# Seven block products instead of eight for nearly all hidden tiles of three FFNs, with the weight sums made by DMA in DRAM

## The reference, cut to what matters

```python
def swiglu_half(x, g, w_up, w_down):
    h = rmsnorm(x, g)
    gate, up = jnp.split(h @ w_up, 2, axis=-1)
    return x + 0.5 * ((jax.nn.silu(gate) * up) @ w_down)

for l in range(DEPTH):
    x = swiglu_half(x, p['ffn1_norm'][l], p['ffn1_w_up'][l], p['ffn1_w_down'][l])
    y, st = mixer(rmsnorm(x, p['mix_norm'][l]), l, lb_all[l], p, tuple(s[l] for s in states))
    x = x + y
    x = swiglu_half(x, p['ffn2_norm'][l], p['ffn2_w_up'][l], p['ffn2_w_down'][l])
```

## Time and profile before

| | |
|---|---|
| Time, median of 3 runs | 3029.66 us (3028.21 to 3030.39) |
| Profiled execution | 3033.17 us, span 3031.4 us |
| TensorE | 2964.1 us busy, 98%, 23664 matmuls |
| VectorE | 1602.5 us busy, 53% |
| ScalarE | 786.5 us busy, 26% |
| GpSimd | 1752.3 us busy, 58% |
| DMA | 271.22 MB, 89 GB/s |

### The profile page before, as it was taken

One profiled execution on the slowest core, in us unless ns is written; L12 is line 12 of the kernel. 1 busy time (PEld: TensorE's weight loads), 2 busy tenths in 40 slices (PEclk: granted clock), 3 DMA queues, 4 the chain that ended last, 5 costly groups with the idle time before them and its releaser, 6 DMA issues.

```text
span 3031.4 us, 65367 instructions
## 1 busy us (share of the span) xinstructions
PE 2964.1 (98%) x23664; PEld 2876.5 (95%) x23664; DVE 1602.5 (53%) x2155; ACT 786.5 (26%) x1296; POOL 1752.3 (58%) x1604
## 2 busy tenths in 40 slices
PE   7999999999999999999999999999999999999998
PEld 7999999989988999999999999999898889999998
DVE  7563665535323467364674736745353245673646
ACT  4221232031232324131241312321303323331212
POOL 5666575545543575656666665654545445766665
PEclk9999999999999999999999999999999999999999
DMA  3232232232221332222232221322312123322231
GB/s 135 79 111 87 70 127 77 67 106 68 82 70 60 106 118 100 88 86 101 74 105 84 90 98 65 125 71 66 114 63 86 63 75 112 108 89 101 80 108 68
DMA packets 115174, 271.22 MB, mean 89 GB/s; under 512 B 9240, under 2 KB 53152, under 8 KB 114720
## 3 DMA queue, kind: packets, MB, share of 16 engines
q1 hardware_dynamic: 65088, 231.76, 22.7%
q10 hardware_dynamic: 49888, 36.71, 4.0%
HBM read 249.92 MB, written 18.52 MB: 89 GB/s over the span
## 4 chain that ended last, share of the span: by engine, by line
PE 88%; DVE 6%; issue 2%; ACT 2%; POOL 1%; ACTq 0%; DMA 0%; PEld 0%; DVEq 0%; POOLq 0%
PE dense L536 64%; PE SA L584 8%; PE SB L584 6%; PE SA L712 1%; PE SA L797 1%; PE SA L698 1%; PE SA L641 1%; PE SA L781 1%; PE SB L793 1%; DVE tmp L1241 1%; DVE Hl L1246 1%; POOL Wl L484 0%; PE SA L683 0%; PE SA L784 0%; PE SA L630 0%
## 5 line engine op out<-in xcount | busy, mean ns | idle before, releaser
L482 POOL TENSOR_SCALAR Wh<-raw 128x512 fp32r<-128x512 f32 x740 | 542.5, 733 | 1037.2 <-PEq L541 935.5
L484 POOL TENSOR_TENSOR Wl<-raw,Wh 128x512 fp32r<-128x512 f32 x740 | 1021.2, 1380 | 61.7
L536 PE MATMUL dense<-Hh,Wh 128*128 128x272 f32 x3104 | 663.0, 295 | 23.6 <-DVE Hl L1232 10.1
L536 PE MATMUL dense<-Hh,Wl 128*128 128x272 f32 x3104 | 648.4, 291 | 0.0
L536 PE MATMUL dense<-Hl,Wh 128*128 128x272 f32 x3104 | 647.9, 290 | 0.0
L536 PEld LDWEIGHTS dense<-Hh,Wh 128*128 128x128 f32 x3104 | 493.7, 191 | 34.8 <-issue 17.6
L536 PEld LDWEIGHTS dense<-Hl,Wh 128*128 128x128 f32 x3104 | 494.9, 191 | 0.0
L536 PEld LDWEIGHTS dense<-Hh,Wl 128*128 128x128 f32 x3104 | 492.9, 192 | 0.0
L536 PE MATMUL dense<-Ah,Wh 128*128 128x272 f32 x1408 | 290.9, 288 | 4.7 <-DVE Al L1333 4.7
L536 PE MATMUL dense<-Ah,Wl 128*128 128x272 f32 x1408 | 289.5, 288 | 0.0
L536 PE MATMUL dense<-Al,Wh 128*128 128x272 f32 x1408 | 289.2, 287 | 0.0
(11 more groups left out here) (423 smaller groups left out, 5246.9 us busy)
## 6 DMA issues: line engine op xcount, KB each, us to landing
raw<-wst SPq DMA_DIRECT2D x336, 512.0 KB, 3.3
pair<-wst SPq DMA_DIRECT2D x80, 512.0 KB, 4.0
raw<-wst SPq DMA_DIRECT2D x32, 384.0 KB, 2.9
x_keep<-X ACTq DMA_DIRECT2D x2, 2176.0 KB, 8.3
X<-x_keep ACTq DMA_DIRECT2D x16, 272.0 KB, 3.1
sst<-st_h ACTq DMA_DIRECT2D x8, 512.0 KB, 4.5
s_h<-sst ACTq DMA_DIRECT2D x8, 512.0 KB, 3.4
sst<-st_c ACTq DMA_DIRECT2D x8, 512.0 KB, 4.0
```

Source lines behind the costliest of these rows:

```text
L482: pool.tensor_scalar(Wh[:, j, cs], raw[:, j, cs], 1.0, 0.0, ALU.mult, ALU.add).then_inc(glink, 1)
L484: pool.tensor_tensor(Wl[:, j, cs], raw[:, j, cs], f32(Wh[:, j, cs]), ALU.subtract).then_inc(glink, 1)
L536: mm = pe.matmul(dps[slot][:, a, 0:HALF], w[:, ring, w0:w0 + 128], x[:, k, a * HALF:(a + 1) * HALF], start=(k == 0 and n == 0), stop=(k == ...
```

## The change

FFN 0 stays as it was, but for signs: the sums of activations and weights are taken with other signs, and the combination adds or subtracts accordingly. In FFNs 1, 2 and 3 all 20 hidden tiles after the first two are computed with seven products, back to back in groups of 6, 8 and 6 between the tiles of w_down.

For these FFNs VectorE makes no weight sums. Three of the four sums (called W1, W2, W3 here, for S1, S2, S3) are made in a DRAM tensor `w_sums` by DMA transfers that GpSimd issues: per chunk of 6 or 8 hidden tiles three copies and three adding transfers, for FFN 1 during FFN 0, for FFN 2 during the mixer of layer 0, for FFN 3 during that of layer 1. They run on two counters, and GpSimd waits for the last transfer of a counter before it issues the next on it. The sum of all four blocks (S4) is made by GpSimd in SBUF from A12 and S2. SyncE loads A11, A12, S1 and S2 (two transfers of 512 KB) when the five rests of VectorE of the last pair are made, and S3 and A22 (two of 256 KB) when the two rests of GpSimd are. VectorE makes five rests per pair, GpSimd two and the sum. The rounding and the rests of the next pair are put between the steps that combine this pair's products (`products`). The first pair of FFNs 1 and 3 is prepared during the tiles of w_out, that of FFN 2 at the end of FFN 1. The loop over the layers is written out, in Python, on all engines.

The core of the diff (of functions with two versions, the order is SyncE, GpSimd, TensorE, ScalarE, VectorE):

```diff
-FAST = FF_TILES // 2 - 1
+HALF_FAST, FAST = FF_TILES // 2 - 1, FF_TILES - 2
+EXTRA = 2 * (FAST - HALF_FAST)
 FFN_TILES = FFN_PIECES - 2 * FAST
+FFN1_T0 = (-EXTRA, 0)
 UP_AT = (2, 18, 34)
-DOWN_AT = (10, 26, 40)
-FAST_AT = (-1, 3, 7)
+HALF_AT = (-1, 3, 7)
+DOWN_AT = ((4, 12, 20), (10, 26, 40))
+FAST_AT = (0, FF_BLOCK - 2, 2 * FF_BLOCK - 2, FAST)
...
+            def load_seven(f, i):
+
+                if i in FAST_AT:
+                    chunk = 3 * (f - 1) + FAST_AT.index(i) + 1
+                    sp.wait_ge(sum_s, 16 * SUM_S * chunk)
+                    sp.sem_inc(pair_began, 1)
+                    sp.wait_ge(sum_r, 16 * SUM_R * chunk)
+                    sp.sem_inc(pair_began, 1)
+                at, n = gate_piece(f, i), (f - 1) * FAST + i
+                sp.wait_ge(q_lo, ONE + LOW0[f] + i * DVE_LO)
+                sp.sem_inc(pair_began, 1)
+                if n:
+                    sp.wait_ge(sum_four, n)
+                    sp.sem_inc(pair_began, 1)
+                sp.dma_start(pair[:, 0:4:3, :], wst[at, :, :].rearrange("p (a c) -> p a c", a=2)).then_inc(first_in, 16)
+                sp.dma_start(pair[:, S2:S1 + 1, :], w_sums[0:2, n, :, :].rearrange("s p c -> p s c")).then_inc(
+                    first_in, 16)
+                sp.wait_ge(q_lo_pool, ONE + POOL0[f] + i * POOL_LO)
+                sp.dma_start(wsum[:, 0, :], w_sums[2, n, :, :]).then_inc(second_in, 16)
+                sp.dma_start(wsum[:, 2, :], wst[at + 1, :, 512:1024]).then_inc(second_in, 16)
...
+            def ffn(f, p0, d0):
+                for t in range(4):
+                    load(p0 + t, d0 + t, t % 2)
+                load_seven(f, 1)
+                for b, nf in enumerate((FF_BLOCK, FF_BLOCK, FF_LAST)):
+                    for m in range(KT):
+                        if m == 2:
+                            for i in range(FAST_AT[b] + 2, min(FAST_AT[b + 1] + 2, FAST)):
+                                load_seven(f, i)
+                            if b == 2 and f == 1:
+                                load_seven(f + 1, 0)
+                        load(p0 + DOWN_AT[0][b] + m, d0 + 24 * b + 2 * nf + m, m % 2, nf * P)
...
+                    if p == MIX_PIECES - 4:
+                        sp.wait_ge(mix_clear, L + 1)
+                        sp.sem_inc(pair_began, 1)
+                        load_seven(2 * L + 1, 0)
...
+            def sums(f, c):
+
+                i0, i1 = FAST_AT[c // SUM_OPS], FAST_AT[c // SUM_OPS + 1]
+                at, n0, n1 = gate_piece(f, i0), (f - 1) * FAST + i0, (f - 1) * FAST + i1
+                blocks = wst[at:at + 2 * (i1 - i0), :, :].rearrange("(n u) p (h c) -> u h p n c", u=2, h=2)
+                G_a, U_a, U_b = blocks[0, 0], blocks[1, 0], blocks[1, 1]
+                W2, W1, W3 = (w_sums[s, n0:n1, :, :].rearrange("n p c -> p n c") for s in range(3))
+                F2, F1 = (flat(w_sums[s, n0:n1, :, :]) for s in range(2))
+                op = c % SUM_OPS
+                if op in (3, 5):
+                    if sent["r"]:
+                        pool.wait_ge(sum_r, 16 * sent["r"])
+                        pool.sem_inc(sum_began, 1)
+                    if op == 3:
+                        pool.dma_start(W3, G_a).then_inc(sum_r, 16)
+                    else:
+                        pool.dma_start(W3, U_a, accum_op=ALU.add).then_inc(sum_r, 16)
+                    sent["r"] += 1
+                    return
+                if sent["s"]:
+                    pool.wait_ge(sum_s, 16 * sent["s"])
+                    pool.sem_inc(sum_began, 1)
+                if op == 0:
+                    pool.dma_start(W1, U_a).then_inc(sum_s, 16)
+                elif op == 1:
+                    pool.dma_start(W1, U_b, accum_op=ALU.add).then_inc(sum_s, 16)
+                elif op == 2:
+                    pool.dma_start(F2, F1).then_inc(sum_s, 16)
+                else:
+                    pool.dma_start(W2, G_a, accum_op=ALU.add).then_inc(sum_s, 16)
+                sent["s"] += 1
...
+            def lows(f, i):
+
+                n = PAIR0[f] + i - HALF_FAST
+                pool.wait_ge(first_in, n * 32 + 32)
+                pool.sem_inc(sum_began, 1)
+                pool.wait_ge(q_lo_pool, ONE + POOL0[f] + i * POOL_LO)
+                pool.tensor_tensor(wsum[:, 1, :], pair[:, A12, :], pair[:, S2, :], ALU.add).then_inc(sum_four, 1)
+                for q in range(DVE_LO, 7):
+                    pool.wait_ge(q_hi, (PAIR0[f] + i) * 7 + (q + 1))
+                    pool.tensor_tensor(Sl[:, q, :], slot(q), f32(Sh[:, q, :]), ALU.subtract).then_inc(q_lo_pool, 1)
...
+                        one(p0 + UP_AT[b] + 2 * i)
+                        if c < 3 * SUM_OPS:
+                            sums(1, c)
+                        one(p0 + UP_AT[b] + 2 * i + 1)
+                        for q, src in ((S3, pair[:, 2, :]), (S4, wsum[:, 2, :]), (A22, pair[:, 3, :])):
+                            pool.wait_ge(q_hi, (HALF_AT[b] + i) * 7 + (q + 1))
+                            pool.tensor_tensor(Sl[:, q, :], src, f32(Sh[:, q, :]), ALU.subtract).then_inc(q_lo_pool, 1)
+                        if c + 1 < 3 * SUM_OPS:
+                            sums(1, c + 1)
+                        c += 2
...
+            def ffn(f, p0):
+                for t in range(4):
+                    one(p0 + t)
+                for b, nf in enumerate((FF_BLOCK, FF_BLOCK, FF_LAST)):
+                    one(p0 + DOWN_AT[0][b], nf * P)
+                    for i in range(FAST_AT[b] + 1, min(FAST_AT[b + 1] + 1, FAST)):
+                        lows(f, i)
+                    for m in range(1, KT):
+                        one(p0 + DOWN_AT[0][b] + m, nf * P)
+                if f == 1:
+                    lows(f + 1, 0)
...
+                for p in range(MIX_PIECES):
+                    one(PIECE_BASE[L] + MIX_P0 + p, parts=(SINGLE[p],) if p in SINGLE else (0, 1))
+                    if p % 2 and 1 <= p // 2 < 1 + 3 * SUM_OPS:
+                        sums(L + 2, p // 2 - 1)
+                    if p == MIX_PIECES - 2:
+                        lows(2 * L + 1, 0)
...
+                    pe.wait_ge(prod_read, n * 5 + (5 if alternate else 2))
                     for q, out, opens, copied, read, x in (
                             (A11, SA[:, 0, h0], True, 0, 0, (hi[:, 0:4, h0], lo[:, 0:4, h0])),
-                            (S2, SA[:, 1, h0], True, 0, 0, (T[0][1], T[1][1])),
-                            (S1, SB[:, 0, h0], True, 0, 0, (T[0][0], T[1][0])),
+                            (S2, SA[:, 1, h0], True, 0, 3, (T[0][1], T[1][1])),
+                            (S1, SB[:, 0, h0], True, 0, 4, (T[0][0], T[1][0])),
                             (A12, SA[:, 0, h0], False, 1, 0, (hi[:, 4:8, h0], lo[:, 4:8, h0])),
-                            (S3, SA[:, 1, h0], False, 0, 1, (T[0][2], T[1][2])),
+                            (S3, SA[:, 1, h0], False, 0, 6, (T[0][2], T[1][2])),
                             (S4, SB[:, 0, h0], False, 2, 0, (hi[:, 4:8, h1], lo[:, 4:8, h1])),
-                            (A22, SB[:, 1, h0], True, 0, 0, (T[0][3], T[1][3]))):
-                        if q < S3:
-                            pe.wait_ge(q_lo, ONE + n * 4 + (q + 1))
+                            (A22, SB[:, 1, h0], True, 0, 5, (T[0][3], T[1][3]))):
+                        by_dve, by_pool = (HALF_DVE, HALF_POOL) if alternate else (DVE_LO, POOL_LO)
+                        if q < by_dve:
+                            pe.wait_ge(q_lo, ONE + LOW0[f] + i * by_dve + (q + 1))
                         else:
-                            pe.wait_ge(q_lo_pool, ONE + n * 3 + (q - S3 + 1))
+                            pe.wait_ge(q_lo_pool, ONE + POOL0[f] + i * by_pool + (q - by_dve + 1))
+                        if q == S2:
+                            pe.wait_ge(t_lo, L * 8 + (which * 4 + 4))
                         if copied:
                             pe.wait_ge(prod_copy, n * 2 + copied)
                         if read:
-                            pe.wait_ge(prod_read, ONE + n * 5 + read)
+                            pe.wait_ge(prod_read, n * 5 + read)
...
+            def high(f, i, q):
+
+                n = PAIR0[f] + i
+                if q < S3:
+                    act.wait_ge(first_in, (n - HALF_FAST) * 32 + 32)
+                elif q == S4:
+                    act.wait_ge(sum_four, (n - HALF_FAST) + 1)
+                else:
+                    act.wait_ge(second_in, (n - HALF_FAST) * 32 + 32)
+                act.wait_ge(prod_done, n * 7 + (q + 1))
+                act.activation(Sh[:, q, :], slot(q), ACT.Copy).then_inc(q_hi, 1)
...
+                def products(i, a, b, ahead=True):
+
+                    n = PAIR0[f] + a + i
+                    t = L * (2 * FF_TILES) + (which * FF_TILES + 2 + a) + i
+                    j = a % 2
+                    act.wait_ge(prod_read, n * 5 + 3)
+                    act.wait_ge(prod_done, 7 + n * 7 + 1)
```

(90 more changed lines are left out.)

364 lines of the change are left out of this document (193 added, 171 removed).

## The result

The changed kernel takes 3105.4 us (median of 4 runs, 3103.7 to 3106.9), the kernel before 3028.9 (4 runs, 3026.9 to 3030.4): ratio 1.0253, interval 1.0235 to 1.0270. It is 76 us slower; the forecast was 14 slower, with a range that ended at 3090. The profiled execution took 3104.66 us with a span of 3102.6, against 3033.17 and 3031.4 before.

A forecast was written before the change was run, and what follows sets the result against it. TensorE, busy 98%, bounds the kernel; afterwards a per-pair ring of ScalarE and VectorE would. Terms -3 + 4 + 4.5 + 4.5 + 4 = +14 gave 3047 us profiled, 3044 as median; range 2993 to 3090 (8 in 10).

The forecast's parts named there:

- The DRAM sums: Transfers issued by GpSimd beside the first FFN and mixers: +4 us, bounds 0 to 84, an add some 17 us.
- the ring: ScalarE-VectorE wait cycle per pair, through the copy of SA: 9.8 plus 1.65 gives 11.46 us; -3 us for three FFNs.
- Matmuls removed: In three FFNs, ten hidden tiles each go from 96 matmuls to 84: 45.2 us less of TensorE.
- register waits: Counters worked out from loop registers before each wait add 0.1 us per late pair: +4 us over three FFNs.
- Lands 3.7 into it; ScalarE wants it at 5.2: A pair's first load, 4.45 us from issue to landing, was to arrive 3.7 us into the previous pair, in time.
- a ring of 12.2: Pair cycle if loads land at 5.5 us: 236.5 us per FFN against 225.5, +33 us for three.
- Port turns of 1.65 on the ring: G half waits 1.04 us for GpSimd's rest of S4, V x G 0.6 for that of A22.
- Block ends: First down tile waits for the last hidden rest, 6.0 us after the last product: +0.75 at two ends per FFN, +4.5.
- Last w_out tile: GpSimd's sum and rests for the next FFN's first pair delay a split: TensorE waits 2.2 us, twice, +4.5.
- a slot of 12, which the double buffer mostly covers: A DRAM add of some 17 us exceeds the 12 us between issues, but buffering hides most of it.
- (2): Longer pair cycle, or GpSimd held by the DRAM transfers: 3076 us, or 3124 at the upper bound; chance 0.16.
- Rival (1): TensorE stays the bound, pairs take 10.56 us inside the changed FFNs: 2993 us; chance 0.24.

The follow-up runs named there:

- the last kernel: Against the changed kernel: transfers reordered, first load earlier, SA copy first, next-FFN rests later, activation sums earlier, GpSimd's S4/A22 rests dropped after first pairs; 2991.7 us.

## Why the prediction was wrong, point by point

The direction was right, and so was the kind of loss inside the groups (a ring round the pair takes back what the 45 us of matmuls gave). The size was not: +14 against +71.5 on the profiled executions. Three steps failed. The DRAM sums were put at 4 us and the slots between their issues at 12 us, and the first FFN and the mixers lost 30.6, some 22 of them by the sums. The wait for the activation sums at an FFN's start was not in the sum at all and cost some 19. And the ring was laid out with a load that lands in time, after 4.45 us; it took 5.8, came late and was the ring itself, 14 us instead of 1. The terms:

- **Matmuls removed.** TensorE has 360 fewer of them; block firsts at 10.55 confirm the 10.56 of a pair.
- **The ring, 11.46 (-3), and register waits (+4).** Mis-sized, and for another reason. Late pairs took 11.76, so the sum is 13 us short over three FFNs; but the ring was the loads', not the copy of SA's. "Lands 3.7 into it; ScalarE wants it at 5.2" failed: in the pair that begins at 1352.84 the load landed 4.8 in, and ScalarE was free for it at 4.3. Its length too: from the wait satisfied to the landing I took 0.43 of issue and 4.0, 4.45 in all; here the two loads take 0.55 and 0.60 to issue and 5.0 to land, 5.8 from 1351.76 to 1357.6. The earlier trace rows were of loads with whole 4 KB rows; the new ones write blocks of 2 KB rows, the second from two places of the sums. The traffic of the sums is not the reason: in the run without them that load, of the same shape from the weight stream, took 5.1 to land. The ring closes on itself (a late rest of S3 makes a late load), which my per-pair schedule with a fixed load time could not show. That the second pair of a block would take 10.8 (it took 11.76 on average) is the same mistake. No run took the register waits alone. One sum of the rivals was off as well: with the second pair at 10.8, a ring of 12.2 gives 234.9 us per FFN and not 236.5.
- **Port turns of 1.65 on the ring.** In the changed kernel the G half keeps its 0.44, because GpSimd's rest of S4 comes after it. V x G did wait 0.62 for the rest of A22, as forecast, but neither turn was on the path (leaving the rests out: 0). The one that is on it is the sum of four with the rest of A11, 0.55. The mechanism itself is right where VectorE is really late (11.95 with the sum moved). The Trainium skill, SBUF — State Buffer, "Who interferes with whom", has the shared pair held for the whole instruction; it says so of VectorE's two-port modes, and of an operation with two SBUF inputs only that it contends with GpSimd's reads. GpSimd's sum runs from 1357.79 to 1359.08 and VectorE's rest ends at 1359.63, 0.55 later for work of 0.68: the trace again has it free some 0.13 before the end, as the earlier trace rows had.
- **Not in the prediction: the activation sums at an FFN's start.** Without the two dense tiles of the first turn (12 us) TensorE reaches product S2 of the first pair that much earlier, and T is not ready: 23.9 us of waiting, and with the slower clock after it the first pairs are 31.6 us longer than 10.55. The waits that stood in the first turn before went, about 12, so the net is some 19. I had listed what the removed tiles cost and not what else they had covered. This is the largest step that the prediction did not have at all. The wait and what follows it (same columns as the windows above), at 1.2 GHz, 21 matmuls in 4.6 us:

```profile
1180.80:1188.70 7.90, 0.00 (x0) 0.00 (x0) 5.51 (x9) 3.50 (x4) 0.51 (x1) 0.63 0.00 0
1188.80:1193.40 4.60, 4.60 (x21) 4.60 (x22) 2.89 (x5) 2.09 (x4) 0.00 (x0) 0.53 0.00 0
```

- **Block ends (+4.5).** The parts of the three FFNs behind the groups are 4.0 longer, 0.6 at each of the six eight-tile block ends (0.75 forecast). Right; the largest wait of that kind is 1.0.
- **Last w_out tile (+4.5).** The wait was 3.2 instead of 2.2, twice. With the slower clock behind it the stretch of the w_out tiles is 8.7 longer in the two mixers together. Undoing it gave 15, of which that stretch shows 9.8.
- **Sums in DRAM (+4, bounds 0 to 84).** Some 30 by leaving them out, 22 by what the first FFN and the mixers lost without the term above; both inside the bounds. The estimate of an add was good: over its nine transfers the first add takes 16.6 us to land and the copy of as much 9.2:

```profile
L567 POOL DMA_DIRECT2D w_sums<-wst x9: 1394/1412/1534, 62.5 to 2187.4; - x9
...
  POOL w_sums L569: 47.5, 4
...
DMA to landing us min/median/max: 12.5/16.6/23.9
...
L556 POOL DMA_DIRECT2D w_sums<-wst x9: 883/889/970, 88.8 to 2222.9; - x9
...
DMA to landing us min/median/max: 8.9/9.2/12.3
```

(The numbers behind the counts are ns of issue, least, median, greatest.) The Trainium skill, Collectives: The Full Stack, "The bandwidth ceiling", states half the copy's rate for the adding step of a collective; the trace agrees for these transfers, 1.8 times. What failed is "a slot of 12, which the double buffer mostly covers". In the first FFN, which I had not weighed at all, the two places of issue are unevenly spaced, and GpSimd was back at the counter after 5.9 us:

```profile
62.51 1.42 POOL L567 DMA_DIRECT2D w_sums<-wst  x1
...
67.12 1.28 POOL L532 TENSOR_TENSOR Wl<-raw,Wh 128x512 fp32r<-128x512 f32 x1
79.69 0.58 POOL L569 DMA_DIRECT2D w_sums<-w_sums  x1 [11.30 <-DMA w_sums<-wst]
...
82.75 0.82 PE L649 MATMUL dense<-Hh,Wh 128*128 128x272 f32 x2 [6.60 <-POOLq L534]
```

An 11.3 us wait of GpSimd's became 6.6 of TensorE's, and at 1.2 GHz after it (14 matmuls from 82.7 to 86.0) the whole group took 31.43 instead of 22.55.

Together: late pairs 14 (with the register waits and the -3), first pairs net 19, block ends 4.0, a longer start of the third FFN 1.5, first FFN and mixers 30.6: 69 of the 71.5. Of the rivals, (2) came nearest in its number (3076 to 3124) and named both mechanisms, a ring near 12 and GpSimd held by the sums; I gave it 0.16. Its ring was priced for a load of 5.5 us, and the load took 5.8. Rival (1), TensorE as the bound, came near only in the last kernel (late pairs 10.67).

What stays open: why a late pair still takes 10.67 against 10.55 without the rests (there ScalarE's rounding waited for the first load in 27 pairs, 12.2 us in all, which was not tested), where the 14 us that don't add went, and why the gains in the first FFN and the mixers, measured one by one, come to more than these stages had lost. What the lower clock cost behind each gap was read from windows; no run took it away alone.

## What to carry to other kernels

When work leaves the bounding engine, list everything that the removed time had covered, at the start and end of the stretch as well as in its steady turn, and lay the steady turn out as closed rings with the loads in them: which release lets the next load go, and what does that release wait for. Give each buffer its own release: one count on one semaphore, late because it covered a buffer that the load did not write, cost 38 us here. A long transfer is cheap or dear by what its issuer does next: here it paid not to issue a second one on a counter right behind an add (25 us).
